# Stacking the sample's new value rows, moving three value steps, other cuts of the final output, and gating the opening's weight loads on the landing of x

## The reference, cut to what matters

```python
for l in range(DEPTH):                                  # DEPTH = 2
    x = x + 0.5 * swiglu(rms(x, norm_ffn1[l]), gate1[l], up1[l], down1[l])
    z = rms(x, norm_mix[l]) @ w_in[l]                   # q, k, v of 3 dilated groups, of the sink branch, 2 gates
    A = softmax-combined dilated attention of 3 groups  # prompt: band; sample: cached keys/values + 8 new rows
    B = windowed attention with sinks                   # the same, one group
    x = x + (sigmoid(gA) * (A @ w_branch_a) + sigmoid(gB) * (B @ w_branch_b)) @ w_out[l]
    x = x + 0.5 * swiglu(rms(x, norm_ffn2[l]), gate2[l], up2[l], down2[l])
y = rms(x, norm_final)
```

## Time and profile before

| | before |
|---|---|
| median of 3 runs | 1472.85 us |
| the profiled execution, its own time | 1472.82 us |
| its span in the trace | 1471.0 us |
| TensorE busy (matmul) | 1456.0 us, 99% |
| VectorE / ScalarE / GpSimd busy | 54% / 45% / 24% |
| mean DMA rate | 238 GB/s |

### The profile page before, as it was taken

How to read it: one execution, slowest core, us unless ns; L and a number is a source line. 1 busy time by engine, 2 the same in 40 slices (tenths; PEclk the granted TensorE clock), 3 DMA queues, 4 the chain that set the end, 5 groups by cost and what they waited for, 6 DMA issues and landing times.

```text
span 1471.0 us, 31019 instructions
## 1 busy us (share of the span) xinstructions
PE 1456.0 (99%) x11408; PEld 1415.5 (96%) x11408; DVE 794.2 (54%) x1281; ACT 668.7 (45%) x1109; POOL 350.0 (24%) x349
## 2 busy tenths in 40 slices
PE   9999999999999999999999999999999999999997
PEld 9999999999889999999999999999898899999997
DVE  5555445855445755544455554477554466555443
ACT  6444344444554544434454443444445445444342
POOL 1322212212115232220122221132121163222200
PEclk9999999999999999999999999999999999999999
DMA  8985566898674798547788846669877558885563
GB/s 311 349 287 177 168 202 201 320 325 283 226 257 135 249 330 295 178 137 206 221 314 293 293 147 183 202 203 334 287 262 273 183 169 293 310 290 156 156 195 112
DMA packets 94979, 349.80 MB, mean 238 GB/s; under 512 B 12336, under 2 KB 23856, under 8 KB 92208
## 3 DMA queue, kind: packets, MB, share of 16 engines
q1 hardware_dynamic: 94752, 348.64, 70.8%
q10 hardware_dynamic: 144, 0.03, 0.0%
HBM read 343.51 MB, written 94.37 MB: 298 GB/s over the span
## 4 chain that ended last, share of the span: by engine, by line
PE 93%; POOL 2%; DVE 2%; ACT 1%; issue 1%; DMA 0%; SPq 0%; DVEq 0%; ACTq 0%; POOLq 0%
PE ps L633 29%; PE ps L634 28%; PE ps L635 28%; PE ps L881 2%; PE ps L895 2%; POOL ma L1582 1%; PE ps L817 1%; PE ps L732 1%; PE ps L781 1%; POOL mlo L1585 0%; PE ps L742 0%; DMA x<-in_x 0%; PE ps L806 0%; ACT whi L1022 0%; PE ps L845 0%
## 5 line engine op out<-in xcount | busy, mean ns | idle before, releaser
L1244 DVE TENSOR_TENSOR wlo<-raw,whi 128x1024 fp32r<-128x1024 f32 (+2 forms) x414 | 485.4, 1173 | 381.7 <-ACT whi L1022 381.3
L633 PE MATMUL ps<-xhi,whi 128*128 128x320 f32 x2048 | 641.7, 313 | 1.0 <-DVE wlo L1482 0.6
L635 PE MATMUL ps<-xhi,wlo 128*128 128x320 f32 x2048 | 632.7, 309 | 0.0
L634 PE MATMUL ps<-xlo,whi 128*128 128x320 f32 x2048 | 632.6, 309 | 0.0
L1022 ACT ACTIVATE whi<-raw 128x1024 fp32r<-128x1024 f32 (+2 forms) x414 | 397.7, 963 | 304.7 <-PE ps L635 300.6
L633 PEld LDWEIGHTS ps<-xhi,whi 128*128 128x128 f32 x2048 | 384.4, 188 | 12.6 <-issue 9.8
L634 PEld LDWEIGHTS ps<-xlo,whi 128*128 128x128 f32 x2048 | 384.6, 188 | 0.5
L635 PEld LDWEIGHTS ps<-xhi,wlo 128*128 128x128 f32 x2048 | 384.4, 188 | 0.0
L633 PE MATMUL ps<-act_hi,whi 128*128 128x320 f32 x704 | 217.5, 309 | 0.0
L634 PE MATMUL ps<-act_lo,whi 128*128 128x320 f32 x704 | 217.5, 309 | 0.0
L635 PE MATMUL ps<-act_hi,wlo 128*128 128x320 f32 x704 | 217.5, 309 | 0.0
(11 more groups left out here) (154 smaller groups left out, 1194.9 us busy)
## 6 DMA issues: line engine op xcount, KB each, us to landing
out_new_a_sample<-in_cache_a SPq DMA_DIRECT2D x128, 510.0 KB, 5.3
raw<-in_ffn_gate SPq DMA_DIRECT2D x87, 512.0 KB, 3.7
raw<-in_ffn_up SPq DMA_DIRECT2D x87, 512.0 KB, 4.5
raw<-in_w_in SPq DMA_DIRECT2D x80, 512.0 KB, 5.3
kvc<-in_kcache SPq DMA_DIRECT2D x52, 512.0 KB, 6.5
kvc<-in_vcache SPq DMA_DIRECT2D x52, 512.0 KB, 5.5
raw<-in_ffn_down SPq DMA_DIRECT2D x64, 384.0 KB, 3.2
raw<-in_ffn_down SPq DMA_DIRECT2D x64, 320.0 KB, 3.0
```

The source lines that it names most:

```text
L633: pe.matmul(out, w0, hi, start=first, stop=False)
L634: pe.matmul(out, w0, lo, start=False, stop=False)
L635: return pe.matmul(out, w1, hi, start=False, stop=last)
L1244: nc.vector.tensor_tensor(wlo[:, (base + s) % RING, 0:tiles * P], raw[:, (base + s) % RAW, 0:tiles * P], whi[:, (base + s) % RING, 0:tiles ...
```

## The change

Four edits. (1) The value steps of items 0, 2 and 5 move in `BEATS`: from beat 14 to 15, from 20 to 21, and from 27 to 28. (2) The sample's new value rows of the three dilated groups are stacked along the partitions (`vnew` 96 x 2 x 256, group g at partition 32 g; the sink branch gets its own `vnb`), so that one transposition of 96 columns replaces three of 32, and 4 products over 96 rows replace 12 over 32. (3) The last scaling and stores are cut 3, 2, 2, 1 blocks instead of 2, 2, 2, 2. (4) In the opening, SyncE waits for quarter 0 of `x` before it issues `b` 0, for quarter 1 before `b` 1, and for quarter 2 before `w` 2.

```diff
+LOAD_AFTER = {("b", 0): 0, ("b", 1): 1, ("w", 2): 2}
+YPARTS = ((0, 3), (3, 5), (5, 7), (7, 8))
...
-BEATS = {10: "S0", 12: "T0 S1a", 13: "S1b", 14: "O0", 15: "T1a", 16: "T1b S2", 18: "T2 O1 S3a", 19: "S3b", 20: "O2",
-         21: "T3a", 22: "T3b S4", 23: "O3", 24: "T4 S5", 26: "T5 O4 S6", 27: "O5", 28: "T6 S7", 30: "T7 O6 S8",
+BEATS = {10: "S0", 12: "T0 S1a", 13: "S1b", 15: "T1a O0", 16: "T1b S2", 18: "T2 O1 S3a", 19: "S3b",
+         21: "T3a O2", 22: "T3b S4", 23: "O3", 24: "T4 S5", 26: "T5 O4 S6", 28: "T6 O5 S7", 30: "T7 O6 S8",
...
+            vnew = sb("vnew", [NG * HALF, 2, 2 * P], F32, att)
+            vnb = sb("vnb", [HALF, 2, P], F32, att)
...
             for part, n in LOADS:
+                if (part, n) in LOAD_AFTER:
+                    sp.wait_ge(x_in[LOAD_AFTER[part, n]], 16)
                 if part == "x":
...
                             pe.transpose(ps[:, BK_T, n * P:(n + 1) * P], e[:, o:o + P], ident)
-                            mm = pe.transpose(ps[0:HALF, *new_place(n, 1)], e[:, on:on + HALF], ident)
+                            if kind == "SB":
+                                mm = pe.transpose(ps[0:HALF, *new_place(n, 1)], e[:, o + P:o + N_SB], ident)
+                        if kind == "SA":
+                            mm = pe.transpose(ps[0:NG * HALF, *new_place(0, 1)], e[:, NG * P:N_SA], ident)
...
-                        for g in range(NG):
-                            for b in range(4):
-                                mm = pe.matmul(ps[HALF * b:HALF * (b + 1), BK_KV, 2 * P * c:2 * P * (c + 1)],
-                                               ptn[:, g * P + HALF * b:g * P + HALF * (b + 1)],
-                                               vnew[:, c, v_slot(g, 0) * P:(v_slot(g, 0) + 2) * P],
-                                               start=g == 0 and c == 0, stop=False, skip_group_check=True)
+                        for b in range(4):
+                            mm = pe.matmul(ps[HALF * b:HALF * (b + 1), BK_KV, 2 * P * c:2 * P * (c + 1)],
+                                           ptn[:, HALF * b:HALF * (b + 1)], vnew[:, c, :],
+                                           start=c == 0, stop=False, skip_group_check=True)
...
-            for n in range(XPARTS):
-                m = slice(n * KD // XPARTS, (n + 1) * KD // XPARTS)
+            for part in YPARTS:
+                m = slice(*part)
                 sp.wait_ge(y_done, m.stop)
```

More of the change, by code:

```diff
@@ L286, in build @@
             vtok = sb("vtok", [P, 2, 7 * P], F32, att)
-            vnew = sb("vnew", [HALF, 2, 7 * P], F32, att)
+            vnew = sb("vnew", [NG * HALF, 2, 2 * P], F32, att)
+            vnb = sb("vnb", [HALF, 2, P], F32, att)
             kst = sb("kst", [P, KST, 3 * P], F32, att)
@@ L294, in build @@
             pts = sb("pts", [P, 2 * NG * SEQ], F32, att)
-            ptn = sb("ptn", [HALF, 4 * P], F32, att)
+            ptn = sb("ptn", [NG * HALF, 4 * P], F32, att)
             sts = sb("sts", [P, N_SA], F32, att)
@@ L442, in skips_first_rows, with new_rows @@
             return kind == "k" and g in (0, 3)
+        def new_rows(g, c):
+            return vnew[HALF * g:HALF * (g + 1), :, c * P:(c + 1) * P] if g < NG else vnb[:, :, :]
         def new_place(first, count):
@@ L543, in store_kv @@
                     src, done = vtok[:, :, cols], v_out
-                    parts = [(slice(4 * half, 4 * half + 4), vnew[:, half, cols]) for half in range(2)]
+                    parts = [(slice(4 * half, 4 * half + 4), new_rows(g, c)[:, half, :]) for half in range(2)]
                 t0 = 0 if g in (1, 2) else 1
@@ L616, in _ @@
                 ffn_loads(L, 1)
[L617 to L618 removed]
+            for part in YPARTS:
+                m = slice(*part)
                 sp.wait_ge(y_done, m.stop)
                 sp.dma_start(a["y"][:, m, :], x[:, m, :]).then_inc(y_out, 16)
[L621 removed]
+            sp.wait_ge(y_out, 16 * len(YPARTS))
             sp.wait_ge(copy_out, 16 * DEPTH * (4 * 2 * NB + 2 * KD + 4 * 2))
@@ L827, in values @@
                                 pe.matmul(ps[r, BK_O, h * P:(h + 1) * P],
-                                          vnew[:, h, 6 * P + HD * j:6 * P + HD * (j + 1)],
-                                          ptn[:, n * P:(n + 1) * P], start=True, stop=False)
+                                          vnb[:, h, HD * j:HD * (j + 1)],
+                                          ptn[0:HALF, n * P:(n + 1) * P], start=True, stop=False)
                             for b in range(4):
@@ L1128, in mixer_act @@
                                                  ps[:, BK_ROWS, 0:2 * P].rearrange("p (t f) -> p t f", t=2), ACT.Copy)
-                            nc.scalar.activation(vnew[:, :, v0:v0 + P],
-                                                 ps[0:HALF, BK_ROWS, 2 * P:4 * P].rearrange("p (t f) -> p t f", t=2),
-                                                 ACT.Copy).then_inc(kvtok_done, 1)
+                            nc.scalar.activation(new_rows(g, c),
+                                                 ps[0:HALF, BK_ROWS, 2 * P:4 * P].rearrange(
+                                                     "p (t f) -> p t f", t=2), ACT.Copy).then_inc(kvtok_done, 1)
                     elif kind == "G":
@@ L1159, in mixer_act @@
                                 act.wait_ge(s_new, L * 2 + 1)
-                            nc.scalar.activation(ptn[:, 0:NG * P], ps[0:HALF, *new_place(0, NG)], ACT.Copy)
+                            nc.scalar.activation(ptn[:, 0:P], ps[0:NG * HALF, *new_place(0, 1)], ACT.Copy)
                             src = ps[:, BK_T, :]
@@ L1176, in mixer_act @@
                                 act.wait_ge(s_new, L * 2 + 2)
-                                nc.scalar.activation(ptn[:, :], ps[0:HALF, *new_place(0, 4)], ACT.Copy)
+                                nc.scalar.activation(ptn[0:HALF, :], ps[0:HALF, *new_place(0, 4)], ACT.Copy)
                             w = {"A": 2 * NG * P, "B": 4 * (t + 1) * P, "SB": 4 * P}[what]
@@ L1510, in _ @@
             dve.wait_ge(xhi_done, (3 * DEPTH + 1) * KD)
[L1511 to L1514, removed]
+            for m0, m1 in YPARTS:
+                m = slice(m0, m1)
+                nc.vector.tensor_tensor(x[:, m, :], xg[:, m, :], strided(ps[:, BK_S, 0:TOK], 0, ((0, m1 - m0), (1, TOK))),
+                                        ALU.mult).then_inc(y_done, m1 - m0)
         @block.gpsimd
```

1 line of the change is left out of this document (removed).

## The result

The changed kernel takes 1465.52 us, the median of 5 runs (1464.73 to 1465.83), against 1472.84 us of the kernel before in the same comparison (5 runs, 1472.41 to 1473.51): a ratio of 0.995 with an interval of 0.9937 to 0.9962. The forecast was 1465.6 us. The profiled execution took 1465.52 us, so its rows stand for the median; its span is 1463.7 us.

The account below looks back on a forecast made before the run. TensorE was taken as the bound, busy 1456.0 of 1471.0 us. Terms -3.0 - 3.8 - 0.9 + 0.2 + 0 + 0.3 = -7.2 took 1472.8 to 1465.6 us, range 1464.3 to 1467.4.

Parts of the forecast that it names:

- The moved value steps: Mixer: values placed a unit later no longer wait for the `vnew` copy, and no new wait appears; -3.0 us.
- the junctions: Mixer: values behind transposes cost +0.7, vanished junctions of small products give -0.5; together +0.2 us, bounds -0.3 and +0.7.
- Fewer products: Mixer: 8 passes over 96 rows replace 24, at 60 ns each, at two items in two layers; -3.8 us.
- Fewer transposes: Mixer: two transposes fewer at each of four places, 0.11 us apart; -0.9 us.
- The rival with 96 rows that don't overlap: Mixer: 96-row products run one after the other, +6.4 instead of -3.8 us, so 1475.8 us; chance 0.03.
- the four terms: Mixer: moved steps -3.0, fewer products -3.8, fewer transposes -0.9 and junctions +0.2 us.
- The last stores: End: first store waits for three blocks instead of two while DMA is saturated; +0.3 us, bounds -0.4 and +0.4.
- The opening: Start: queue keeps issue order, so the waits bring quarter 2 no sooner; 0 us, bounds -1.5 and +3.9.
- the gates do help: Opening: quarters of `x` land sooner since fewer loads compete; 0.4 to 1.5 us gained, 1464.1 to 1465.2; chance 0.17.
- what the prediction named as wrong: Signs against it: quarter 2 more than 0.5 us sooner, TensorE idle at unit 2, or passes 0.1 us or more apart.
- unit 2 late: Opening: unit 2's load takes over 4.3 us and TensorE stands; 0.4 to 1.0 late, 1466.0 to 1466.6; chance 0.16.
- the near one of the earlier trace: Opening: a 512 KB load with little queued takes 3.5 us, so unit 2 lands at 13.0; among other traffic 8.2.

Follow-up runs that it names:

- hold_all: Changed kernel with one wait only: every load behind quarter 2 of `x` is issued only once quarter 2 has landed; 1467.68 us, one run.
- b_gates: Changed kernel without the wait ahead of unit 2's load, the two early waits kept; 1464.77 us, ratio 0.9947.
- w_gate: Changed kernel with only the wait ahead of unit 2's load, the two early waits removed; 1465.36 us, one run.
- after: The changed kernel itself with all four edits, in its first comparison against the kernel before; 1465.52 us, ratio 0.995.
- after_again: The changed kernel unchanged, measured once more in a second comparison; 1465.19 us, ratio 0.9953.
- gates_only: Kernel before with nothing but the three waits of the opening added; 1472.95 us, ratio 1.0002.
- b_even_w16: Changed kernel without unit 2's wait, with four equal last stores and 32 warm-up passes instead of 40; 1463.97 us, ratio 0.994.
- even_y: Changed kernel with the last rows of y scaled and stored in four equal pieces, as before; 1465.31 us, one run.
- b_even: Changed kernel without the wait ahead of unit 2's load and with four equal last stores; 1464.99 us, ratio 0.9945.
- beats_only: Kernel before with only the new order of the mixer's value steps (`BEATS`); 1469.99 us, ratio 0.9981.
- stack_only: Kernel before with only the stacked new value rows; 1468.81 us, ratio 0.9974.

## Why the prediction was right, point by point

**The moved value steps** were put at -3.0 with +0.2 for the junctions, -2.8 together; the order alone measures -3.12. The wait is gone and nothing took its place, as the working said. As far as one execution tells, the junctions cost nothing or a little less than nothing; +0.2 was too dear.

**Fewer products** were put at -3.8: 0.86 us are saved at each of four places (1.43 - 0.57), -3.4. A pass costs 71 ns for the 60 taken from L895, because each group ends with a fixed piece that 24 or 32 passes spread and 8 do not. By the starts of the single passes in the trace, four start within 0.02 us, the next four 0.22 to 0.24 later (54 to 60 ns a pass), and from the last four to the next work it is 0.32 us in the kernel before and 0.33 in the changed one. The 16 passes that are gone were four steps of 0.216, which is the 0.86. **Fewer transposes** were put at -0.9, and 0.22 at four places is that. The rival with 96 rows that don't overlap is out: four of them start together. What the working missed is the 0.5 that the stacked copy adds to the wait, which the moved steps hid.

From unit 2 to the last norm the four terms gave -7.5. Nine executions with both edits have 1437.06 to 1437.27 us there, three with neither edit 1444.52 to 1444.64: -7.4.

**The last stores** were put at +0.3 and measure 0.3 to 0.4 in every execution. The first store is issued 1.18 us after the scaling has begun (1458.63 - 1457.45), before 0.85 (1465.95 - 1465.10), and the DMA engines are then busy nearly without a gap to the end of the transfer, as in the earlier trace rows: it starts later and ends later.

**The opening** is the step that failed, though its value of 0 came out. The sentence "the queue keeps the order of issue, and there is nothing to take out of the way" is wrong. The packet sizes of the earlier trace rows say what most packets of one microsecond are; they don't say that quarter 2 is complete. The test on rows of the kernel before would have been to count: 2.38 MB moved by 9.47 us, with 1.51 up to and with quarter 2. The rule cited from the Trainium skill ("DMA: Bandwidth & Descriptors", section "Queues, rings and completion order") was read too widely. It speaks of the ring that each of the 16 engines has for a queue, and the same section says that completion is not first in, first out for the issuing engine. My reading of it is that a load has landed only when the slowest engine has done its share, while the others are already in the loads behind.

The trace agrees with that reading, since it records each of the 16 counts that a load adds to its semaphore. In the kernel before, the counts of quarter 2 come from 6.90 to 9.44 us, 15 of them by 7.86, and the first counts of the three loads behind it (`b` 0, quarter 3, `b` 1) come at 7.76, 8.64 and 9.30, ahead of its last. The first count of quarter 2 hardly moves, 6.5 to 6.9 in all 14 profiles. From there to the last it takes 1.86 to 2.70 us in the six without the early waits, 1.21 to 1.75 in the seven with them, and 0.92 in hold_all. So holding back the loads behind does bring the one ahead sooner, by shortening the tail of its shares. Why fewer loads behind make the late shares less late is not shown. By bytes, 0.35 to 0.45 MB of later loads are in when quarter 2 is used in the four executions with all waits, 0.47 to 0.87 in the five with none.

The working also looked at the wrong wait. It held that the early two hold little back and that only the third, ahead of units 2 and 3, could free quarter 2; b_gates and w_gate show the reverse. The issues of `b` 0, `b` 1 and unit 2 by SyncE in the kernel before:

```profile
3.09 0.43 SPq L609 DMA_DIRECT2D raw<-in_ffn_gate  x1
...
4.04 0.71 SPq L609 DMA_DIRECT2D raw<-in_ffn_up  x1
4.79 0.61 SPq L609 DMA_DIRECT2D raw<-in_ffn_gate  x1
```

In the changed kernel, behind their waits:

```profile
3.88 0.33 SPq L619 DMA_DIRECT2D raw<-in_ffn_gate  x1
...
6.21 0.33 SPq L619 DMA_DIRECT2D raw<-in_ffn_up  x1
7.81 0.33 SPq L619 DMA_DIRECT2D raw<-in_ffn_gate  x1
```

So the early two waits hold `b` 0 back by 0.8 us and `b` 1 by 2.2, and that is enough. This is what the rival "the gates do help" expected, and what the prediction named as wrong (quarter 2 over 0.5 us sooner, TensorE idle at unit 2) is what the trace shows.

The gain was given back by the other rival, unit 2 late. I let the load issued behind quarter 2 land after 3.5 us, the near one of the earlier trace rows. In the four executions with all waits it is issued at 7.81 to 8.12 and `whi` starts 4.7 to 5.25 us later, behind loads that had been held back themselves; in w_gate, where they had not, it is issued at 8.73 and `whi` starts 3.8 later.

Where quarter 2 comes early, the table reads as two terms: unit 2's first product comes 2.37 us after its `whi`, or some 7.1 us after the first product, whichever is later. In after, after_again and gates_only the former ends last (12.77 + 2.37 = 15.14 for 15.15), and in b_even_w16 too, where quarter 1 came late; in even_y, b_gates and b_even the latter. Over the executions without waits unit 2's product starts at 15.74 on average (five), with all three at 15.42 (four): 0.3 us, too little for the times to show, and smaller than the spread of the four (15.11 to 15.99). The 0.93 of the first comparison was two single executions, one late and one early.

**What was not in the sum.** In the changed kernel's profiled execution L1023 took 1.44 us where L1013 took 0.81 in the kernel before, at a granted clock of 0.51, the lower level of 1.2 GHz. The windows of the changed kernel (us; TensorE busy and passes; granted clock; DMA) show it:

```profile
1453.00:1455.00 2.00, 0.73 (x8) 1.00 0.00 0
1455.00:1457.00 2.00, 1.44 (x2) 0.51 0.00 0
```

TensorE had been in the short matmuls of the last norm since the last unit's products, with idle gaps of 0.69 and 1.15 us. The same gaps stand in the executions that kept 2.4 GHz. Of the 14 profiles five have the slow last matmul (after, gates_only, beats_only, stack_only, hold_all), among them kernels with both orders, with and without waits, and after_again, the same kernel as after, has not. It is worth 0.6 us and belongs to the execution, not to the change. What decides it stays open.

So the sum's -7.2 stands for: mixer -7.4, stores +0.3, opening about -0.3 (an average over four and five executions, not told from nothing by the times), which is -7.4 against a measured -7.3 and -7.4 in two comparisons. The mixer's and the stores' terms were right in kind and nearly in size. That the first comparison gave 1465.52 for 1465.6 is in part luck: the 0.93 won in that opening and the 0.63 lost at that slow matmul were both outside the sum.

## What to carry to other kernels

A load that stands ahead in its queue is not safe from those behind it: add up the bytes moved by the time it is used and compare them with the bytes up to and with it in the order of issue. A surplus says that later loads were under way before it had landed; what they cost it, only a run with them held back tells. Before holding back a load, find who is waiting for that one next; here 1 us won on `x` became a wait at unit 2. Two edits that each touch one wait should be tried alone too: here the stacking by itself lengthens the wait that the new order removes. And where the terms are under 1 us, compare two or more executions of the same kernel before reading one, since the ends of this program move by 0.6 to 1.5 us on their own.

## What was not expected of the hardware

The warm-up is the widest scatter of the opening. The same 40 passes took 6.11 us in after and 7.65 in even_y; the rows are TensorE's first of each, in that order:

```profile
1.46 6.11 PE L1007 MATMUL ps<-ones 128*128 128x128 f32 x40 [1.46 <-DVE eps L1488]
```

```profile
1.46 7.65 PE L1007 MATMUL ps<-ones 128*128 128x128 f32 x40 [1.46 <-DVE eps L1488]
```

In the windows of the same two, from 6 to 7 us, the changed kernel (first) has 12 passes in a microsecond and even_y (second) still 7, while the column of the granted clock reads 1.00 in both:

```profile
6.00:7.00 1.00, 1.00 (x12) 1.00 1.02 347
```

```profile
6.00:7.00 1.00, 1.00 (x7) 1.00 0.96 328
```

So the pace rises from 7 to 12 passes in a microsecond at a moment that lies between 4 and over 7 us in these executions, and the first product, right behind the warm-up, moves between 7.33 and 8.87 with it. The granted clock of the profile doesn't show the slow stretch at the start, though it shows the one at the end. What sets the slow pace and the moment is not shown.
